# Gates of two branches computed beside their branch jobs, in one staging slot, with the head flips behind the last gate

## The chip, the cores and the metric

One core of a Trainium2 chip runs the whole program. The metric is the device time of one execution in microseconds, here the median of three. An execution with the hardware profiler gives the trace from which all rows come.

## The reference

A trunk of two layers over 768 tokens (two sequences of 256 and 512) with 1024 channels, all in float32. Of each layer, this is the part that matters here:

```python
proj = rms_norm(x, norm1_g) @ w_in            # q/k/v of three mixers, and gate_pre
o_a = dilated window attention(proj)          # 384 wide
o_b = bidirectional mLSTM(proj)               # 512 wide
o_c = rms_norm(differential attention(proj))  # 512 wide, 4 heads of 128, in two sequences
gates = sigmoid(gate_pre).reshape(Bn, S, 3, 1024)
y_a, y_b, y_c = o_a @ w_branch[:384], o_b @ w_branch[384:896], o_c @ w_branch[896:]
mixed = gates[:, :, 0] * y_a + gates[:, :, 1] * y_b + gates[:, :, 2] * y_c
x = x + mixed @ w_out
x = x + (silu(hg) * hu) @ w_ffn_out           # hg, hu = split(rms_norm(x) @ w_ffn_in)
```

## The kernel before

Every float32 product is made of three matmuls on rounded parts: high by high, high by low, low by high. `wh` and `wl` hold the parts of weights, `xh`, `xl` and `oh`, `ol` those of activations (transposed: channels on partitions, tokens along the row). ScalarE makes the high part by a copy (L1080), VectorE the low one by a subtraction (L1357); weights come in sub-chunks of 512 KB through three raw buffers `wraw`, issued by SyncE.

The work of a layer is a list `STEPS`, made by `schedule()` before the program is built. Each engine goes through the same list and does its share of each step, so the list is the order on every engine. It mixes two kinds of steps.

*Dense steps* are the large products. Each takes one of three PSUM banks in turn (L1758 to L1760 for the matmuls). `piece` steps are the projections; `gate b d q` is the product for block d (128 channels) of branch b's gate, for half q (384 tokens), 24 matmuls, which ScalarE turns into a sigmoid by three activations (L1089 to L1091) in one of three slots of `stage`; `branch b d q` is the product of branch b's output with its rows of w_branch, 9 matmuls for b = 0, 12 for the others; `turn 1 t` transposes token tile t of the mLSTM output, loaded by `turn_load` into a half of `wide`; `wout t h` is the last product.

*Side steps* are the small ones of the mixers, on the other five banks. `schedule()` puts one in when enough dense cost has gone by since the last (the `GAP` numbers). For the differential attention a unit is one tile of 128 queries of one head: `c_score` (L1975), a maximum on VectorE (L1651), two exponentials on ScalarE (L1264), `c_mix` (L1659 to L1662), `c_turn` (L1985), `c_out` (L1997). A head is opened by `c_fold` (L1961, transposes of q and k) and closed by `c_norm` (L1672 to L1680). `c_flip` (L2006) transposes the normed head into the operand of branch 2, in `xh[:, 4:8]`, whose rest VectorE makes (L1687). It overwrites the normalized input of the layer, so no flip may come before the last gate.

All 48 gate jobs stand ahead of the branch jobs, the last 32 of them beside mLSTM and differential units. Each gate is stored to `gate_t` in HBM by GpSimd's queue (L821). Of the branch jobs, those of branches 0 and 1 do this: GpSimd loads the gate back (`load_gate`, L840), VectorE multiplies the bank by it in place (L1423), GpSimd stores the product to `mix_t` (L870), for branch 1 as an accumulating store. Five slots serve for it (`gated`). In branch 2 the product is summed with the part loaded from `mix_t` (`load_part`, L851, three slots; L1430), and ScalarE and VectorE split the sum for w_out (L1147, L1410). `x` itself is loaded back from `x_save` (L880) for the last eight jobs of branch 2. GpSimd's queue is in order, so a load behind a wait holds all that follow:

```python
elif i >= GSLOTS:
    wait_mix_stored(i - GSLOTS)
```

In `mix(step)` of job i, `load_gate(i + 4)` is called first, so it waits for the store of job i - 1 to have landed.

## Time and profile before

| | us |
|---|---|
| median of three executions (3585.18 to 3595.86) | 3586.19 |
| the profiled execution | 3596.83 |
| its span, first to last instruction | 3595.2 |
| TensorE busy in the span | 3224.1 |
| VectorE, ScalarE, GpSimd busy | 1572.4, 1170.7, 508.5 |
| mean granted share of TensorE's clock | 0.96 |

Busy time is the time in which an engine carries out instructions. A wait is written down for the instruction that stood behind it, with the instruction or transfer that ended it. The layer loop runs twice, so most things stand in the trace twice.

### The profile page before, as it was taken

How to read it: one execution, taken by the hardware profiler on the slowest of the kernel's cores; microseconds unless marked ns; L12 is line 12 of the kernel's file. 1: busy time of each engine (PE TensorE's matmuls, PEld its weight loads, DVE VectorE, ACT ScalarE, POOL GpSimd, SP SyncE). 2: the span in 40 equal slices, each digit the busy share in tenths (PEclk: the TensorE clock that was granted, in tenths of full speed). 3: DMA queues.
4: the chain of work that ended last, by engine and by line, in shares of the span. 5: the costliest groups of instructions: out<-in, count | busy, mean ns of one | idle time of the engine just before them, and what ended most of it. 6: DMA issues, size and time to landing. Idle time of an engine off the chain costs nothing. (4 is left out here: it accounts for less than half of the span.)

```text
span 3595.2 us, 45725 instructions
## 1 busy us (share of the span) xinstructions
PE 3224.1 (90%) x17652; PEld 2940.5 (82%) x17652; DVE 1572.4 (44%) x3225; ACT 1170.7 (33%) x2480; POOL 508.5 (14%) x872
## 2 busy tenths in 40 slices
PE   6799998999866999999978899989998669999998
PEld 6788888787765899999877898877877658999997
DVE  5345245644433334434464442466444243344434
ACT  4334334455511221111143334344555112111111
POOL 0111312221223000000001113222112230000000
PEclk9999999999988999999989999999999889999999
DMA  3434443442256122112033344434323561122111
GB/s 126 136 100 131 126 141 111 126 120 88 88 144 168 47 71 71 55 50 70 30 122 107 107 135 123 139 114 121 115 93 102 133 176 36 59 70 70 58 47 65
DMA packets 273368, 358.63 MB, mean 100 GB/s; under 512 B 27440, under 2 KB 209904, under 8 KB 273176
## 3 DMA queue, kind: packets, MB, share of 16 engines
q1 hardware_dynamic: 214520, 182.59, 17.2%
q0 software_dynamic: 58656, 173.50, 15.7%
q8 instruction: 118, 1.93, 0.2%
q14 instruction: 74, 0.61, 0.1%
HBM read 264.42 MB, written 91.59 MB: 99 GB/s over the span
## 5 line engine op out<-in xcount | busy, mean ns | idle before, releaser
L1758 PE MATMUL ps<-wh,xh 128*128 128x384 f32 (+1 forms) x1440 | 543.8, 378 | 11.2 <-DVE wl L1357 6.6
L1759 PE MATMUL ps<-wl,xh 128*128 128x384 f32 (+1 forms) x1440 | 524.2, 364 | 0.0
L1760 PE MATMUL ps<-wh,xl 128*128 128x384 f32 (+1 forms) x1440 | 524.1, 364 | 0.0
L1758 PE MATMUL ps<-xh,wh 128*128 128x384 f32 (+1 forms) x1184 | 424.1, 358 | 111.3 <-DVE stage L1430 49.6
L1760 PE MATMUL ps<-xh,wl 128*128 128x384 f32 (+1 forms) x1184 | 408.6, 345 | 0.0
L1759 PE MATMUL ps<-xl,wh 128*128 128x384 f32 (+1 forms) x1184 | 408.5, 345 | 0.0
L1357 DVE TENSOR_TENSOR wl<-wraw,wh 128x1024 fp32r<-128x1024 f32 (+2 forms) x210 | 232.5, 1112 | 401.1 <-ACT wh L1080 400.6
L1832 PE MATMUL ps<-xh,wh 128*128 128x384 f32 x1408 | 361.4, 337 | 20.1 <-DVE arena L1745 15.4
L1832 PE MATMUL ps<-xl,wh 128*128 128x384 f32 x1408 | 359.0, 336 | 0.0
L1832 PE MATMUL ps<-xh,wl 128*128 128x384 f32 x1408 | 358.7, 335 | 0.0
L1758 PEld LDWEIGHTS ps<-xh,wh 128*128 128x128 f32 (+1 forms) x1184 | 229.1, 194 | 132.7 <-DVE stage L1423 55.0
L1758 PEld LDWEIGHTS ps<-wh,xh 128*128 128x128 f32 x1440 | 279.9, 194 | 41.5 <-DVE wl L1357 6.7
L1718 DVE SCALAR_TENSOR_TENSOR arena<-arena,ps 128x768 f32<-128x768 f32 x44 | 42.0, 955 | 601.5 <-ACT arena L1319 601.5
L1759 PEld LDWEIGHTS ps<-wl,xh 128*128 128x128 f32 x1440 | 279.1, 194 | 23.7 <-issue 1.4
L1760 PEld LDWEIGHTS ps<-wh,xl 128*128 128x128 f32 x1440 | 277.5, 193 | 25.1
L1832 PEld LDWEIGHTS ps<-xh,wh 128*128 128x128 f32 x1408 | 254.6, 189 | 28.4 <-issue 20.5
L1832 PEld LDWEIGHTS ps<-xl,wh 128*128 128x128 f32 x1408 | 255.8, 189 | 0.0
L1832 PEld LDWEIGHTS ps<-xh,wl 128*128 128x128 f32 x1408 | 255.7, 189 | 0.0
L1760 PE MATMUL ps<-wh,ol 128*128 128x512 f32 x624 | 243.2, 390 | 0.0
L1759 PE MATMUL ps<-wl,oh 128*128 128x512 f32 x624 | 243.1, 390 | 0.0
L1758 PE MATMUL ps<-wh,oh 128*128 128x512 f32 x624 | 242.7, 389 | 0.0
L1319 ACT ACTIVATE arena<-ps 128x768 f32<-128x768 f32 x44 | 35.8, 815 | 615.3 <-PE ps L1832 615.3
(223 smaller groups left out, 5020.5 us busy)
## 6 DMA issues: line engine op xcount, KB each, us to landing
wraw<-in_w_in SPq DMA_DIRECT2D x96, 512.0 KB, 3.8
wraw<-in_w_ffn_in SPq DMA_DIRECT2D x88, 512.0 KB, 4.0
wraw<-in_w_in SPq DMA_DIRECT2D x72, 384.0 KB, 3.6
wraw<-in_w_ffn_out SPq DMA_DIRECT2D x44, 512.0 KB, 3.3
qkv_a<-stage POOLq DMA_DIRECT2D x108, 192.0 KB, 2.2
gate_t<-stage POOLq DMA_DIRECT2D x96, 192.0 KB, 2.2
stage<-gate_t POOLq DMA_DIRECT2D x78, 192.0 KB, 2.7
mix_t<-stage POOLq DMA_DIRECT2D x52, 192.0 KB, 3.6
```

The lines of the kernel that those rows point to most:

```text
L1319: act.activation(f_e[:, ft, :].rearrange("p (h n) -> p h n", h=2), ps[:, 4 * ft:4 * ft + 2, 0:HALF_TOK], ACT.Tanh, scale=0.5).then_inc(f_e ...
L1357: dve.tensor_tensor(wl[:, half, j, 0:w], wraw[:, n % RAW, 0:w], wh[:, half, j, 0:w].bitcast(F32), ALU.subtract).then_inc(w_lo, 1)
L1718: fch.link(dve.scalar_tensor_tensor(e2, e2, 1.0, ps[:, 4 * ft:4 * ft + 2, 0:HALF_TOK], ALU.add, ALU.mult))
L1758: pe.matmul(out, ah, bh, start=first, stop=False)
L1759: pe.matmul(out, ah, bl, start=False, stop=False)
L1760: return pe.matmul(out, al, bh, start=False, stop=last)
L1832: mm = pe.matmul(pair[0:cols, q, 0:HALF_TOK], w[:, half, j, sl_], v[:, k, q * HALF_TOK:(q + 1) * HALF_TOK], start=(k == 0 and w is wh and ...
```

## The change

It orders and places work anew; all products, sigmoids and sums are the same.

1. The gates of branch 2 are computed first, where those of branch 0 were, and stored to `gate_t`, which keeps one branch instead of three. The gates of branches 0 and 1 are not stored: job i's gate is computed, two gates later comes its branch job, and VectorE multiplies the bank by the gate in the staging slot itself. The product is stored to `mix_t` from there, and the slot's next gate waits for this store. Weights come in `mix` chunks of two gate sub-chunks and one of the branch.
2. The turns of branch 1 go to `oh`, `ol` in place of branch 0's operand, behind its last job, since `xh`, `xl` are needed by the gates; they stand in two groups of three.
3. All eight flips follow the last gate, in groups of three, three and two, in four side banks; the heads' outputs get places of their own in the arena. The square of `c_norm` goes to PSUM (`AT_OUT`), so the next head's first `c_out` waits for the reduction of it.
4. Branch 2 has five slots for parts. The first five gates are loaded behind the last `c_norm`, the first five parts during branch 1; `x` is loaded back in its first six jobs, in two groups of three tiles.
5. `GAP_C` is 3.7 instead of 4, and w_out is taken second half first.

```diff
-    gates = [("gate", [("in", 0, 8, COL_GATE + (4 * i + j) * P, P) for j in range(4)]) for i in range(6)]
-    chunks += gates[0:2]
+    gate = lambda b, d: ("in", 0, 8, COL_GATE + (KD * b + d) * P, P)
+    for i in range(2):
+        chunks.append(("gate", [gate(2, 4 * i + j) for j in range(4)]))
     for i in range(3):
         chunks.append(("c", [("in", 2 * j, 2, COL_C + i * C_W, C_W) for j in range(4)]))
-    chunks += gates[2:6]
-    for b, parts in ((0, ((0, 1), (2, 3))), (1, (range(4),)), (2, (range(4),))):
-        for part in parts:
-            chunks.append(("branch", [("branch", *MIX_ROWS[b], 2 * j * P, 2 * P) for j in part]))
-    for h in range(2):
+    for b in range(2):
+        for i in range(4):
+            chunks.append(("mix", [gate(b, 2 * i), gate(b, 2 * i + 1), ("branch", *MIX_ROWS[b], 2 * i * P, 2 * P)]))
+    chunks.append(("branch", [("branch", *MIX_ROWS[2], 2 * j * P, 2 * P) for j in range(4)]))
+    for h in (1, 0):
         chunks.append(("out", [("wout", 2 * j, 2, h * 512, 512) for j in range(4)]))
     return chunks
...
-    if kind == "gate":
-        return C_GATE[(8 * s[1] + s[2]) // 4], s[2] % 4
-    if kind == "branch":
-        b, j = s[1], s[2] // 2
-        return (C_BRANCH + j // 2, j % 2) if b == 0 else (C_BRANCH + 1 + b, j)
+    if kind in ("gate", "branch"):
+        b, d = s[1:3]
+        if b < 2:
+            return C_MIX + 4 * b + d // 2, d % 2 if kind == "gate" else 2
+        return (C_GATE + d // 4, d % 4) if kind == "gate" else (C_BRANCH, d // 2)
     if kind == "wout":
-        return C_OUT + s[2], None
+        return C_OUT + 1 - s[2], None
...
-GAP_A, GAP_B, GAP_C, ROUND = (1, 2, 4, 2.5), (4, 4, 6), 4, 0.45
+GAP_A, GAP_B, GAP_C, ROUND = (1, 2, 4, 2.5), (4, 4, 6), 3.7, 0.45
...
-    dense += [("gate", 0, d, q) for d in range(KD) for q in range(2)]
+    dense += [("gate", 2, d, q) for d in range(KD) for q in range(2)]
     dense += [("piece", c, t) for c in range(C_C, C_C + 3) for t in range(NT)]
-    dense += [("gate", b, d, q) for b in (1, 2) for d in range(KD) for q in range(2)]
-    for d in range(KD):
-        dense += [("branch", 0, d, q) for q in range(2)]
-        if d < NT:
-            dense.append(("turn", 1, d))
-        if d + 2 < NT:
-            dense.append(("turn_load", 1, d + 2))
-    dense += [("branch", 1, d, q) for d in range(KD) for q in range(2)]
+    jobs = [(d, q) for d in range(KD) for q in range(2)]
+    for b in range(2):
+        for i in range(len(jobs) + 2):
+            if i < len(jobs):
+                dense.append(("gate", b, *jobs[i]))
+                if b == 1 and i < 2:
+                    for t in range(3 * i, 3 * i + 3):
+                        dense.append(("turn", 1, t))
+                        if t + 2 < NT:
+                            dense.append(("turn_load", 1, t + 2))
+            if i >= 2:
+                dense.append(("branch", b, *jobs[i - 2]))
     dense += [("branch", 2, d, q) for q in (1, 0) for d in range(KD)]
...
-        if flips and flips[0] in normed and ("gate", 2, KD - 1, 1) in gone and (
+        if flips and flips[0] in normed and ("gate", 1, KD - 1, 1) in gone and ("c_norm", 7) in gone and (
                 len(dense_of(steps)) > max(normed[flips[0]], flipped) or not dense or not side and dense[0] == ("branch", 2, 0, 0)):
             steps.append(("c_flip", flips.pop(0)))
             gone.add(steps[-1])
-            flipped = len(dense_of(steps))
+            if flips and flips[0] % 3 == 0:
+                flipped = len(dense_of(steps))
             continue
...
+                        if step[0] == "gate" and step[1] < 2:
+                            return
...
-                        if m == len(STAGED) - 1:
-                            wait_stage(m)
-                            for i in range(GSLOTS - 1):
-                                load_gate(i)
-
-                    def wait_mix_stored(i):
-
-                        pool.wait_ge(mix_stored[i % GSLOTS], 16 * (i // GSLOTS + 1))
-
-                    def load_gate(i):
-
-                        _, b, d, q = MIX_LIST[i]
-                        if i - GSLOTS >= MIX_LAST:
-                            pool.wait_ge(r_lo, i - GSLOTS - MIX_LAST + 1)
-                        elif i >= GSLOTS:
-                            wait_mix_stored(i - GSLOTS)
-                        elif i == GSLOTS - 1:
-                            pool.wait_ge(b_dec, len(B_UNITS))
-                        pool.dma_start(gated[i % GSLOTS], gate_t[b, d * P:(d + 1) * P, HALVES[q]]
-                                       ).then_inc(gate_in[i % GSLOTS], 16)
+
+                    def load_gate(j):
+
+                        _, b, d, q = MIX_LIST[MIX_LAST + j]
+                        if j >= GSLOTS:
+                            pool.wait_ge(r_lo, j - GSLOTS + 1)
+                        pool.dma_start(gated[j % GSLOTS], gate_t[d * P:(d + 1) * P, HALVES[q]]).then_inc(gate_in[j % GSLOTS], 16)
...
+
+                    def first_gates():
+
+                        stage_stored(STAGE["gate", 2, KD - 1, 1])
+                        pool.wait_ge(c_tr, len(C_FOLDS))
+                        pool.wait_ge(c_ptr, len(C_UNITS))
+                        pool.wait_ge(c_pv, len(C_UNITS))
+                        for j in range(GSLOTS):
+                            load_gate(j)
+
+                    parts = []
+
+                    def first_parts(ready):
+
+                        while len(parts) < PSLOTS and 2 * len(parts) + 1 <= ready:
+                            load_part(len(parts))
+                            parts.append(ready)
 
...
+                        pool.wait_ge(mixed, i + 1)
                         if b < 2:
-                            pool.wait_ge(mixed, i + 1)
+                            m = STAGE["gate", b, d, q]
                             if b:
-                                wait_mix_stored(MIXES["branch", 0, d, q])
+                                stage_stored(STAGE["gate", 0, d, q])
                             add = {"accum_op": ALU.add} if b else {}
-                            pool.dma_start(mix_t[d * P:(d + 1) * P, HALVES[q]], gated[i % GSLOTS], **add
-                                           ).then_inc(mix_stored[i % GSLOTS], 16)
+                            pool.dma_start(mix_t[d * P:(d + 1) * P, HALVES[q]], stage[:, m % SLOTS, 0:HALF_TOK], **add
+                                           ).then_inc(stored[m % SLOTS], 16)
+                            if b and STEPS.index(("c_norm", 7)) < STEPS.index(step):
+                                first_parts(i - 2 * KD - 2)
                             return
                         j = i - MIX_LAST
-                        if j + PSLOTS - 1 < 2 * KD:
-                            load_part(j + PSLOTS - 1)
-                        if KD <= j < KD + NT:
-                            t = FFN_TILES[j - KD]
-                            if j == KD:
-                                pool.wait_ge(c_flo, len(C_HEADS))
-                            pool.dma_start(x[:, t, :], x_save[t * P:(t + 1) * P, :]).then_inc(x_back, 16)
+                        if j == 0:
+                            first_parts(2 * KD)
+                            pool.wait_ge(c_flo, len(C_HEADS))
+                        if j + PSLOTS < 2 * KD:
+                            load_part(j + PSLOTS)
+                        if 1 <= j and j - 1 + GSLOTS < 2 * KD:
+                            load_gate(j - 1 + GSLOTS)
+                        if j < NT:
+                            t = FFN_TILES[j]
+                            pool.dma_start(x[:, t, :], x_save[t * P:(t + 1) * P, :]).then_inc(x_back[j // 3], 16)
...
+                        elif kind == "c_norm" and step[1] + 1 == len(C_HEADS):
+                            first_gates()
                         elif kind == "turn_load":
                             load_turn(*step[1:])
+                        elif kind == "turn" and step[1:] == (1, NT - 1):
+                            pool.wait_ge(d_done, INDEX["turn", 1, NT - 1] + 1)
+                            pool.dma_start(wide[:, :], io["norm2_g"][layer].partition_broadcast(P)
+                                           ).then_inc(gain2_in, 16)
...
                         elif kind == "branch":
                             i = MIXES[step]
-                            e = gated[i % GSLOTS]
-                            dve.wait_ge(gate_in[i % GSLOTS], 16 * (i // GSLOTS + 1))
+                            j = i - MIX_LAST
+                            if j < 0:
+                                g = ("gate", *step[1:])
+                                e = stage[:, STAGE[g] % SLOTS, 0:HALF_TOK]
+                                dve.wait_ge(act_staged, PLAIN[g] + 1)
+                            else:
+                                e = gated[j % GSLOTS]
+                                dve.wait_ge(gate_in[j % GSLOTS], 16 * (j // GSLOTS + 1))
                             dve.wait_ge(d_done, n + 1)
                             ins = dve.tensor_tensor(e, ps_bank(n)[:, 0:HALF_TOK], e, ALU.mult)
-                            if i < MIX_LAST:
+                            if j < 0:
                                 ins.then_inc(mixed, 1)
                             else:
-                                j = i - MIX_LAST
                                 chain.link(ins)
                                 dve.wait_ge(part_in[j % PSLOTS], 16 * (j // PSLOTS + 1))
                                 dve.tensor_tensor(e, e, part_mix[j % PSLOTS], ALU.add).then_inc(mixed, 1)
...
                             dve.wait_ge(c_pv, C_LAST[H] + 1)
-                            if H >= 4:
-                                dve.wait_ge(c_fl, H - 3)
                             chain.link(dve.reciprocal(unit_s[:, 44:44 + n], c_z[:, H % 3, 0:n]))
                             dve.tensor_tensor(o, side[:, AT_OUT:AT_OUT + n * P].rearrange("p (t e) -> p t e", t=n),
                                               spread(unit_s[:, 44:44 + n]), ALU.mult).then_inc(c_ov, 1)
                             dve.wait_ge(co_sq, H + 1)
-                            dve.tensor_reduce(unit_s[:, 48:48 + n], c_tmp[:, 0:n * P].rearrange("p (h e) -> p h e", e=P), AX_X,
+                            dve.tensor_reduce(unit_s[:, 48:48 + n], side[:, AT_OUT:AT_OUT + n * P].rearrange("p (h e) -> p h e", e=P), AX_X,
                                               ALU.add).then_inc(co_ss, 1)
                             dve.wait_ge(co_rs, H + 1)
...
                             if H and t == 0:
-                                pe.wait_ge(c_ov, H)
+                                pe.wait_ge(co_ss, H)
...
                             pe.wait_ge(co_n, H + 1)
-                            flip_bank_free(pe, step)
+                            if H == 0:
+                                pe.wait_ge(c_ex, 2 * len(C_UNITS))
+                                pe.wait_ge(c_pt, len(C_UNITS))
+                                pe.wait_ge(co_ss, len(C_HEADS))
+                            if H >= 4:
+                                pe.wait_ge(c_flo, H - 3)
                             for t in range(n):
-                                mm = pe.transpose(side[:, AT_FOLD + t * P:AT_FOLD + (t + 1) * P], c_o[:, H % 4, t, :],
-                                                  ident[:, :])
+                                mm = pe.transpose(flip_bank(H)[:, t * P:(t + 1) * P], c_o[H][:, t, :], ident[:, :])
                             mm.then_inc(c_fl, 1)
```

Two places in the orders of the engines. First GpSimd's queue at the end of branch 1 and the start of branch 2, before; `stage` and `arena` hold the gates there, L840 are their loads, L870 the stores of products, L851 the parts.

```order
L840 DMA arena<-gate_t 128x384
L870 DMA mix_t<-stage 128x384
L840 DMA stage<-gate_t 128x384
L870 DMA mix_t<-stage 128x384
L851 DMA arena<-mix_t 128x384 x2
L861 ISA
L861 DMA wide<-in_norm_g 128x1024
L840 DMA stage<-gate_t 128x384
L851 DMA arena<-mix_t 128x384
```

In the changed program the same place reads as follows; L873 are the stores of products, L836 the loads of branch 2's gates, L844 the parts, L888 the tiles of x.

```order
L873 DMA mix_t<-stage 128x384 x2
L836 DMA arena<-gate_t 128x384 x5
L873 DMA mix_t<-stage 128x384
L844 DMA arena<-mix_t 128x384 x3
L873 DMA mix_t<-stage 128x384 x2
L844 DMA arena<-mix_t 128x384
L873 DMA mix_t<-stage 128x384 x2
L844 DMA arena<-mix_t 128x384
L873 DMA mix_t<-stage 128x384 x4
L844 DMA arena<-mix_t 128x384
L888 DMA arena<-x_save 128x1024
L844 DMA arena<-mix_t 128x384
L836 DMA arena<-gate_t 128x384
```

The gate loads ahead of each store are gone; the loads of gates and parts for branch 2 stand between the stores of branch 1, and x follows the first job of branch 2 instead of the ninth.

Second, TensorE's order at the turns, whose operand is `wide`. Before, the first turn, between branch jobs of branch 0, flips and a unit:

```order
L2006 MATMUL ps<-ident,arena 128x128 x4
L1814 MATMUL ps<-ident,wide 128x128 x4
L2006 MATMUL ps<-ident,arena 128x128 x4
L1975 MATMUL ps<-arena 128x256 x2
L1985 MATMUL ps<-ident,arena 128x128 x2
L1997 MATMUL ps<-arena 128x128 x2
```

In the changed program the first group stands between two units of the differential attention (L1993 the scores, L2003 and L2015 its turn and output, L1979 a fold):

```order
L1993 MATMUL ps<-arena 128x512 x2
L2003 MATMUL ps<-ident,arena 128x128 x4
L2015 MATMUL ps<-arena 128x128 x4
L1979 MATMUL ps<-ident,arena 128x128 x4
L1830 MATMUL ps<-ident,wide 128x128 x12
L1993 MATMUL ps<-arena 128x512 x2
L2003 MATMUL ps<-ident,arena 128x128 x4
```

Three turns of four transposes have become one run of twelve. The second and third load of `wide` follow the first and second turn in GpSimd's queue.

## Rows read from the trace of the kernel before

**Rows 1.** The page, busy time and share of the span.

```profile
PE 3224.1 (90%) x17652; PEld 2940.5 (82%) x17652; DVE 1572.4 (44%) x3225; ACT 1170.7 (33%) x2480; POOL 508.5 (14%) x872
```

**Rows 2.** TensorE, waits of the whole run: who for whom; us, times, longest.

```profile
PE ps L1758 <- DVE stage L1430: 51.1, 11, 19.8
...
PE ps L1758 <- DVE stage L1423: 46.4, 22, 4.4
...
PE ps L1975 <- ACT arena L1264: 20.3, 22, 2.0
...
PE ps L1758 <- DVE arena L1423: 12.6, 8, 3.9
...
PE ps L2006 <- DVE arena L1680: 11.0, 4, 3.5
...
PE ps L1961 <- DMA arena<-qkv_c: 9.7, 2, 4.8
PE ps L2006 <- DVE xl L1687: 8.1, 6, 2.5
...
PE ps L1961 <- DVE xl L1687: 5.2, 2, 2.6
...
PE ps L1758 <- DVE arena L1430: 2.6, 2, 1.5
```

**Rows 3.** Stretches: length, PE, PEld, DVE, ACT, POOL busy, PEclk, DMA share, GB/s.

```profile
808.00:967.00 159.00, 146.25 (x870) 125.99 (x869) 71.18 (x125) 87.81 (x207) 26.50 (x42) 0.99 0.26 81
967.00:1040.00 73.00, 57.10 (x303) 52.32 (x302) 35.91 (x72) 24.17 (x53) 22.26 (x41) 0.88 0.54 164
1040.00:1121.00 81.00, 37.51 (x156) 33.05 (x156) 11.20 (x17) 0.00 (x0) 25.13 (x36) 0.77 0.54 103
1121.00:1160.00 39.00, 31.70 (x155) 29.82 (x156) 24.03 (x43) 10.64 (x17) 16.57 (x32) 0.91 0.71 231
2521.00:2945.00 424.00, 341.19 (x1875) 302.88 (x1874) 176.71 (x331) 166.17 (x368) 105.99 (x174) 0.93 0.43 120
```

**Rows 4.** Timeline of TensorE in branch 2 (start, length).

```profile
1121.65 0.69 PE L1758 MATMUL ps<-xh,wh 128*128 128x384 f32 x1 [19.83 <-DVE stage L1430]
...
1130.86 0.44 PE L1758 MATMUL ps<-xh,wh 128*128 128x384 f32 x1 [0.95 <-DVE stage L1430]
...
1134.97 0.34 PE L1760 MATMUL ps<-xh,wl 128*128 128x384 f32 x1
```

**Rows 5.** Timeline of GpSimd in branch 1.

```profile
1096.18 0.56 POOL L840 DMA_DIRECT2D stage<-gate_t  x1 [3.67 <-DMA mix_t<-stage]
1096.72 0.89 POOL L870 DMA_DIRECT2D mix_t<-stage  x1
1101.10 0.57 POOL L840 DMA_DIRECT2D stage<-gate_t  x1 [3.49 <-DMA mix_t<-stage]
```

**Rows 6.** Timeline of VectorE, the product of a branch-2 job.

```profile
1124.27 0.55 DVE L1423 TENSOR_TENSOR stage<-ps,stage 128x384 f32<-128x384 f32 x1
```

**Rows 7.** DMA issues of the branch stretches, median us to landing.

```profile
mix_t<-stage POOLq DMA_DIRECT2D x26, 192.0 KB, 3.6
...
wide<-o_tok POOLq DMA_DIRECT2D x4, 256.0 KB, 3.6
```

**Rows 8.** Timeline of GpSimd at the first fold.

```profile
791.29 0.56 POOL L821 DMA_DIRECT2D gate_t<-stage  x1 [6.71 <-ACT stage L1091]
```

**Rows 9.** Timeline beside one unit of the differential attention.

```profile
870.33 0.69 ACT L1264 ACTIVATE arena<-ps,c_s 128x512 f32<-128x512 f32 x1 [2.25 <-DVE c_s L1651]
...
872.15 0.50 ACT L1089 ACTIVATE stage<-ps 128x384 f32<-128x384 f32 x1
...
873.67 1.04 ACT L1080 ACTIVATE wh<-wraw 128x1024 fp32r<-128x1024 f32 x1
...
874.74 1.23 DVE L1357 TENSOR_TENSOR wl<-wraw,wh 128x1024 fp32r<-128x1024 f32 x1 [4.44 <-ACT wh L1080]
...
877.00 1.22 DVE L1651 TENSOR_REDUCE c_s<-ps 128x2 f32<-128x1024 f32 x1
...
878.25 0.69 ACT L1264 ACTIVATE arena<-ps,c_s 128x512 f32<-128x512 f32 x1 [3.54 <-DVE c_s L1651]
```

**Rows 10.** Stretch with loads of x in flight.

```profile
1150.00:1155.00 5.00, 2.26 (x14) 1.94 (x13) 1.26 (x3) 0.53 (x1) 1.17 (x3) 1.00 1.01 374
```

More of the change, by code:

```diff
@@ L60 @@
 GSLOTS = 5
-PSLOTS = 3
+PSLOTS = 5
 SUB = 1024
@@ L297, in side_needs @@
         return ("piece", C_C + 2, NT - 1)
-    if kind == "c_norm" and s[1] >= 4:
-        return ("c_flip", s[1] - 4)
     return None
@@ L363, in schedule @@
             steps.append(("ffn_split",))
-        if done < NT and i >= WOUT.index((FFN_TILES[done], 1)):
+        if done < NT and i >= WOUT_END[FFN_TILES[done]]:
             steps.append(("rms", NT + done))
@@ L382 @@
 STAGE = {s: m for m, s in enumerate(STAGED)}
-FLIP_BANK = [s for s in STEPS if s[0] in ("c_fold", "c_flip")]
 MIXES = {s: i for i, s in enumerate([s for s in DENSE if s[0] == "branch"])}
@@ L519, in build @@
         b_og = area("b", 4 * P).rearrange("p (t e) -> p t e", t=4)
+        b_o = area("b", 4 * P).rearrange("p (t e) -> p t e", t=4)
+        early = used["bg"] = used["b"]
+        b_w = area("b", 2 * B_W).rearrange("p (i h e) -> p i h e", i=2, h=B_H)
+        b_u = area("b", 4 * P)
+        b_q = area("b", 4 * P)
+        b_k = area("b", 4 * P)
+        b_c = area("b", 4 * P + 2)
         b_d = area("b", 2 * 10 * P).rearrange("p (d n) -> p d n", d=2)
-        b_o = area("b", 4 * P).rearrange("p (t e) -> p t e", t=4)
         b_nb = area("b", 2 * 2 * 4 * P).rearrange("p (r d n) -> p r d n", r=2, d=2)
@@ L559, in build @@
         stored = [sem(f"stored{i}") for i in range(SLOTS)]
-        mix_stored = [sem(f"mix_stored{i}") for i in range(GSLOTS)]
         gate_in = [sem(f"gate_in{i}") for i in range(GSLOTS)]
@@ L564, in build @@
         n_rstd, n_xn, n_tr, n_hi, n_lo = (sem(x) for x in ("n_rstd", "n_xn", "n_tr", "n_hi", "n_lo"))
-        x_saved, x_back = sem("x_saved"), sem("x_back")
+        x_saved, x_back = sem("x_saved"), [sem(f"x_back{i}") for i in range(2)]
         t_in = [sem(f"t_in{i}") for i in range(2)]
@@ L655, in build, with flip_bank @@
         AT_TURN, AT_OUT, AT_FOLD = 1024, 1536, 2048
-        def flip_bank_free(eng, step):
-            before = [s[0] for s in FLIP_BANK[:FLIP_BANK.index(step)]]
-            if "c_fold" in before:
-                eng.wait_ge(c_qkt, before.count("c_fold"))
-            if "c_flip" in before:
-                eng.wait_ge(c_flo, before.count("c_flip"))
+        def flip_bank(H):
+            return side[:, 512 * (H % 4):512 * (H % 4 + 1)]
         def mix_rows(hi, d):
@@ L856, in mix @@
                         i = MIXES[step]
-                        if b == 2 and i == MIX_LAST:
-                            for r in range(PSLOTS - 1):
-                                load_part(r)
-                            pool.wait_ge(d_done, INDEX["turn", 1, NT - 1] + 1)
-                            pool.dma_start(wide[:, :], io["norm2_g"][layer].partition_broadcast(P)
-                                           ).then_inc(gain2_in, 16)
-                        if i + GSLOTS - 1 < len(MIXES):
-                            load_gate(i + GSLOTS - 1)
+                        pool.wait_ge(mixed, i + 1)
@@ L1956, in side_step @@
                             pe.wait_ge(c_lin, 32 * (H + 1))
-                            flip_bank_free(pe, step)
+                            i = C_FOLDS.index(step)
+                            if i:
+                                pe.wait_ge(c_qkt, i)
                             at = AT_FOLD
```

82 lines of the change are left out of this document (39 added, 43 removed).

## Prediction

> **What bounds the kernel now.** I read the page's busy shares first: TensorE 3224 of 3595 us, no other engine over half [rows 1]. So the time is TensorE's work plus the 371 us in which it does nothing, and the question is which of these idle stretches the change reaches. The wait table of TensorE for the whole run lists them by what ended them [rows 2]. Two lines belong to the branch jobs: the wait for L1423 (product of a bank and a gate; 46.4 + 12.6 us) and for L1430 (sum with the part loaded back; 51.1 + 2.6 us). That is 113 us. Then 19.1 us before head flips (L2006), 5.2 us of a fold (L1961) behind a flip's rest in the same bank, 9.7 us of a fold behind a load of qkv_c, 20.3 us of score jobs behind the exponentials of the unit before.
>
> Next I cut one layer into stretches [rows 3]. Idle time is length minus PE busy: 12.8 us in the gates beside differential units, then 15.9, 43.5 and 7.3 us in the three stretches of branch jobs, 79 us; with half of the 9.7 us above it is 84 for the stretch that the change reorders. Layer 2 in one row: 424.0 - 341.2 = 83. The granted clock falls as well: 0.88, 0.77 and 0.91 in the branch stretches against 0.99 ahead of them. The wait of 1121.65 us (19.8 us long) and the rows behind it show what TensorE does at full speed: 24 matmuls from 1130.86 to 1134.97, a step of 0.179 us, so 12 matmuls (a branch job of 4 row blocks) are 2.15 us, 9 are 1.6 and a gate's 24 are 4.3 [rows 4].
>
> Why the branch jobs wait is in GpSimd's queue [rows 5]. Ahead of each product it issues the load of a gate into a slot whose mix store must have landed (3.5 us of idle time before each load), then the next store. One job passes every 4.9 us (1096.18 to 1101.10) where TensorE needs 2.15.
>
> **What is removed.** Branches 0 and 1 get their gate from a staging slot that ScalarE filled one or two jobs earlier; the 32 gate stores, the 32 gate loads and the load-behind-store loop are gone in each layer. The jobs of the loop now have a gate job of 4.3 us between them, so a pair takes 6.4 us of TensorE against a chain of product 0.55, issue 0.6 to 0.9 and landing 3.6 [rows 5 to 7]. I remove the 113 us of L1423 and L1430. The 19.8 us wait goes with them: it was the last accumulating stores, read back by the first parts. Parts 0 to 4 are now requested between branch-1 jobs.
>
> Flips: eight in four banks behind the last gate. Their heads are normed long before, and no fold shares their bank. Of 19.1 + 5.2 us I take away 22; the fifth flip still waits for the first one's rest.
>
> Fold behind its load: in the program's order GpSimd asks for qkv_c right behind a gate store, and this store, of 791.29, waited 6.7 us for the sigmoid [rows 8]. That store no longer exists, and the product that stands in its place comes earlier. 9.7 us go.
>
> Slow clock: the three branch stretches hold 57.1 + 37.5 + 31.7 = 126.3 us of busy time [rows 3]. Their 48 branch jobs have 528 matmuls, 94.5 us at 0.179, and the turns, flips and last unit pieces some 9 (an estimate from their counts at the 0.1 to 0.3 us that such pieces take): 23 us a layer are slow clock and restarts. With gates between the jobs I let 8 remain: -15 a layer, -30.
>
> **What is added.** (a) Turns of branch 1: they stood one between two pairs of branch jobs each; now they stand in two groups of three, and `wide` has two halves. The third of a group waits for a load that GpSimd issues only when the first is done. Issue to landing is 3.6 us for such a load [rows 7], less the 0.5 us of the turn between and plus a semaphore: 3.3 us, four times: +13. The Trainium skill ("DMA: Bandwidth & Descriptors", section on the anatomy of one DMA) gives about 2.0 us plus bytes over 436 GB/s, for 256 KB an estimate of 2.6 us; by it this term would be +9. The row is used.
>
> (b) Units of the differential attention beside shorter jobs. The loop that can hold them is in [rows 9]: exponentials at 870.33, sigmoid 872.15, weight split on ScalarE 873.67 and VectorE 874.74, maximum 877.00, next exponentials 878.25: 7.9 us. The score jobs that waited did so 20.3 / 22 = 0.9 us [rows 2], so TensorE's own work in such a period is 7.0: a gate of 4.3 and a unit of 2.7. In the branch-0 part a unit now has a gate and a branch job beside it (8.6 us), which covers the loop. In the branch-1 part units stand alternately beside a gate and beside a branch job of 2.15 us. Only 3 sub-chunks are split for 8 jobs there; about five splits fall beside gates (0.9 each) and one beside a branch job, where the loop without a sigmoid but with a product is some 7.0 against 4.9 (2.1). That is 7 us a layer against today's 10; I add 8 a layer for the ends of heads, where the next head's first output product now waits for a reduction too, for the turns' evacuations and for slots: 5 a layer net, +10. Bounds: 0, and all 16 units of a layer at 7.9 instead of 4.3 / 2 + 2.15 / 2 + 2.7 = 5.9 us, +64.
>
> (c) Branch 2: gates, parts (five slots now) and the six x tiles (512 KB each) are all asked for in its first jobs. About 11 gates, 11 parts and 6 tiles are 7.4 MB, with 2 MB of w_out in the 34 us of its 16 jobs: 280 GB/s. The trace moves 374 GB/s with x tiles in the queue and 231 over the stretch [rows 3, 10]. By job 10 it must have some 5.7 MB + 1 MB in 21 us, 320 GB/s. I take +4 a layer, +8 (bounds 0 and, at 231 GB/s, 8 us a layer). The staging slots cost nothing on TensorE: the gate that reuses a slot ends 4.3 us after the branch job, the store lands 0.55 + 0.2 + 3.6 us after it, so ScalarE waits some tenths, and TensorE wants the gate's bank 6.4 us later.
>
> Edits at nothing: gate 2 in gate 0's early place, the halves of w_out exchanged, other arena places (same bytes); the square in PSUM (0.6 us before, hidden like now).
>
> **The sum.** -113 - 22 - 10 - 30 + 13 + 10 + 8 = -144; I give back 6 for new small starts between 64 alternating jobs: -138. The profiled execution took 3596.8 us (span 3595.2), 10.6 over the median of 3586.2; so 3459 profiled and 3448 as median.
>
> **Rivals.** *The unit loop binds* (7%): short jobs leave every unit of the branch-1 part to the chain of [rows 9], slot waits of ScalarE lengthen it. Speaks for it that maximum and exponentials stand in one order with split and sigmoid; against, that only three splits fall to eight jobs. +60: 3508.
>
> *The clock stays low* (8%). TensorE's granted clock was 0.99 in the stretch of gates and units with 11 short waits of score jobs (22 in both layers [rows 2]) and 0.77 where it waited 3.5 us at every job [rows 3, 5]. If many short waits were enough, the 30 us would not come back and the gates would lose as much again: +50, 3498. The Trainium skill has such a rule ("TensorE: Matmul & The Clock Gate", on the second failure mode): frequent short idling between groups of matmuls makes the clock swing. The row of 0.99 with 12.8 us of short waits does not bear it out here.
>
> *Everything overlaps* (8%): turns' loads and x tiles are hidden, the clock returns whole: 3448 - 35 = 3413.
>
> *Slower: three slots are too few* (2%). A slot now holds a gate through sigmoid, waiting, product and store. If the landing came so late that ScalarE passed 4 us of wait on to TensorE's bank, every gate of branches 0 and 1 would be held; with 64 gates it decides from 138 / 64 = 2.2 us each, a landing of about 10 us. The rows have 3.6. At 3 us each: 3448 + 192 = 3640.
>
> *It moves nothing* (2%): the idle time turns up again in front of branch 2; 3586.
>
> **The numbers.** The forecast has 73%, its own range 3425 to 3475 from the bounds of (a), (b), (c) and the clock. The range for 8 in 10 takes in the clock rival: 3418 to 3498. A measurement of this kernel tells some 0.3% (11 us) from no change. Faster 0.96, same 0.02, slower 0.02.
>
> **What would show it.** Right: the L1423 wait under 10 us, L1430 under 15, granted clock above 0.95 from the first gate of branch 0 to w_out, waits of the turns on `wide` of 3 us, four of them. Wrong: score jobs waiting for exponentials over 60 us in total (unit loop), a clock under 0.9 without long waits, sigmoids waiting for slots with TensorE's gates behind them.

## The result, and the profile after

The changed kernel takes 3504.16 us (median of four runs, 3503.35 to 3505.1), the kernel before 3585.68 beside it: a ratio of 0.9767, 95% interval 0.9749 to 0.9785. The prediction was 3448 us with a range of 3418 to 3498. The sign and the terms removed were right, the gain was 82 us and not 138, and the time lies 6 us outside the range. The profiled execution took 3503.35 us, the one of before 3596.8: 93.5 us by the two traces.

The page of the changed kernel, the row of busy times:

```profile
PE 3213.1 (92%) x17652; PEld 2936.1 (84%) x17652; DVE 1568.7 (45%) x3225; ACT 1168.7 (33%) x2480; POOL 438.1 (13%) x744
```

The span is 3501.7 us. Beside [rows 1] TensorE is idle for 288.6 us instead of 371.1 (-82.5) and busy for 11 us less. The prediction had 108 us less idle time (all its terms but the clock) and 30 us less busy time. TensorE's waits in the whole run of the changed kernel (who for whom; us, times, longest):

```profile
PE ps L1993 <- ACT arena L1278: 39.7, 16, 4.6
PE ps L1965 <- DVE arena L1615: 29.5, 10, 4.6
...
PE ps L1830 <- DMA wide<-o_tok: 13.0, 4, 3.6
...
PE ps L1950 <- ACT arena L1226: 7.1, 3, 3.3
PE ps L1774 <- ACT stage L1105: 6.8, 4, 2.7
...
PE ps L2029 <- DVE xl L1703: 5.6, 3, 2.8
...
PE ps L1774 <- DVE arena L1449: 3.6, 4, 1.5
PE ps L1774 <- DVE stage L1443: 3.4, 5, 1.3
```

Against [rows 2] (its L1423 and L1430 are now L1443 and L1449): the 113 us of branch jobs are 7.0 (the last two rows), the head flips' 19.1 us are 5.6, the fold behind its load is gone, the turns wait 13.0 us as computed. New or longer are the score jobs (L1993, 39.7 instead of 20.3), the mLSTM's output and score jobs (L1965 29.5, L1950 7.1) and jobs that wait for a gate's last activation (L1105, 6.8). All of these wait for ScalarE or VectorE, so I asked what ScalarE waits for. Its waits in the changed kernel:

```profile
ACT stage L1103 <- DMA mix_t<-stage: 135.1, 26, 9.8
ACT arena L1278 <- DVE c_s L1669: 120.5, 40, 5.3
```

A sigmoid (L1103 is its first activation) waits 26 times, 5.2 us on average, until the mix store of its staging slot has landed. The prediction gave this "some tenths". Such a wait begins when ScalarE runs idle, which can be before the gate's bank is ready; counted from when the bank was ready and ScalarE free, the 26 sigmoids are 105 us late, 4.0 on average. The exponentials wait 120.5 us for the maximum. In the kernel before, the same view has no first row, and of the second

```profile
ACT arena L1264 <- DVE c_s L1651: 89.0, 36, 3.5
```

One of the waits for a landing can be followed through four queues. The timeline of the changed kernel (start, length, in brackets the idle time before and who ended it), rows of TensorE's dense jobs left out:

```profile
820.14 0.55 DVE L1443 TENSOR_TENSOR stage<-ps,stage 128x384 f32<-128x384 f32 x1
820.51 0.76 POOL L1045 DMA_DIRECT2D o_tok<-arena  x1 [9.22 <-DVE arena L1648]
822.24 0.56 DVE L1443 TENSOR_TENSOR stage<-ps,stage 128x384 f32<-128x384 f32 x1 [0.42 <-PE ps L1776]
...
823.55 1.09 POOL L998 DMA_DIRECT2D wide<-o_tok  x2 [2.28 <-DMA o_tok<-arena]
...
824.64 1.08 POOL L873 DMA_DIRECT2D mix_t<-stage  x2
...
827.78 0.49 ACT L1103 ACTIVATE stage<-ps 128x384 f32<-128x384 f32 x1 [9.74 <-DMA mix_t<-stage]
...
829.29 0.67 ACT L1278 ACTIVATE arena<-ps,c_s 128x512 f32<-128x512 f32 x1
...
830.86 2.08 PE L1993 MATMUL ps<-arena 64*128 64x512 f32 x4 [4.57 <-ACT arena L1278]
...
832.60 1.04 ACT L1094 ACTIVATE wh<-wraw 128x1024 fp32r<-128x1024 f32 x1
...
833.67 1.23 DVE L1371 TENSOR_TENSOR wl<-wraw,wh 128x1024 fp32r<-128x1024 f32 x1 [10.88 <-ACT wh L1094]
...
835.93 1.22 DVE L1669 TENSOR_REDUCE c_s<-ps 128x2 f32<-128x1024 f32 x1
837.07 0.55 DVE L1443 TENSOR_TENSOR stage<-ps,stage 128x384 f32<-128x384 f32 x1
837.18 0.69 ACT L1278 ACTIVATE arena<-ps,c_s 128x512 f32<-128x512 f32 x1 [3.54 <-DVE c_s L1669]
```

The slot that the sigmoid at 827.78 needs is that of the product at 820.14, whose branch job had ended at 814.76: VectorE had the steps of the mLSTM's output ahead of it. The stores of both products then stand in GpSimd's queue behind the store of that output (820.51) and the loads of two turns, and these loads wait for the output to land. So the mix stores go from 824.64 on, the sigmoid starts at 827.78, the exponentials queued behind it at 829.29, and TensorE's score job has waited 4.57 us. It goes on from there: ScalarE's half of a weight split (L1094) stands behind the sigmoids, VectorE's rest of it (L1371) has waited 10.88 us for that half, and behind the rest stand the maximum of the next unit and the next product. The product's store is what a later sigmoid waits for. By this order it can go in a circle: landing, sigmoid, split, rest, product, store, landing; and the maximum with the exponentials hangs on the same two queues. How much each part costs is for the experiments.

The clock: stretches of the changed kernel (length, PE busy, further engines, PEclk, DMA share, GB/s).

```profile
900.00:1000.00 100.00, 86.81 (x472) 72.95 (x470) 47.47 (x90) 48.06 (x122) 15.51 (x21) 0.86 0.26 64
...
1077.00:1111.00 34.00, 32.24 (x184) 31.43 (x183) 25.79 (x46) 11.14 (x18) 14.98 (x28) 1.00 0.85 285
```

In the stretch 900:1000, turns and units with branch-1 gates, TensorE waits 12.7 us (four score jobs up to 3.2 us, one turn 3.6 us) and is granted 0.86. Inside it:

```profile
905.00:910.00 5.00, 5.00 (x31) 4.43 (x29) 2.23 (x4) 2.88 (x7) 1.43 (x2) 1.00 0.18 52
910.00:917.40 7.40, 3.83 (x28) 2.90 (x24) 4.58 (x7) 4.99 (x13) 1.29 (x2) 0.84 0.23 71
917.40:921.80 4.40, 4.40 (x16) 2.84 (x16) 3.65 (x7) 1.23 (x3) 0.55 (x1) 0.50 0.36 117
```

Busy without a gap TensorE has 1.00; it waits 3.57 us for a turn's load (until 916.44), the clock of 910:917.4 is 0.84, and at 917.4:921.8 it is at 0.50, the level of 1.2 GHz. Over the whole of the reordered part, 731:1111, it is 0.93, where the prediction's sign of being right was above 0.95. Branch 2 (1077:1111) is at 1.00 with 285 GB/s.

### The profile page after: what moved, and what is told of

The parts are those of the page before. It is cut to its first block and busy times, and to the rows that moved or that the text cites. A ratio compares the mean times of both kernels' runs of the same rounds, so it can differ in the third digit from the quotient of the medians.

```text
span 3501.7 us, 45591 instructions
## 1 busy us (share of the span) xinstructions
PE 3213.1 (92%) x17652; PEld 2936.1 (84%) x17652; DVE 1568.7 (45%) x3225; ACT 1168.7 (33%) x2480; POOL 438.1 (13%) x744
## 5 line engine op out<-in xcount | busy, mean ns | idle before, releaser
L1371 DVE TENSOR_TENSOR wl<-wraw,wh 128x1024 fp32r<-128x1024 f32 (+2 forms) x210 | 232.5, 1112 | 484.1 <-ACT wh L1094 483.5
L1774 PE MATMUL ps<-xh,wh 128*128 128x384 f32 (+1 forms) x1056 | 363.2, 344 | 7.0 <-DVE arena L1449 3.6
L1775 PE MATMUL ps<-xl,wh 128*128 128x384 f32 (+1 forms) x1056 | 356.4, 337 | 0.0
L1776 PE MATMUL ps<-xh,wl 128*128 128x384 f32 (+1 forms) x1056 | 356.3, 337 | 0.0
L1776 PEld LDWEIGHTS ps<-wh,xl 128*128 128x128 f32 x1440 | 277.3, 193 | 24.6
L1094 ACT ACTIVATE wh<-wraw 128x1024 fp32r<-128x1024 f32 (+2 forms) x210 | 199.7, 958 | 39.1 <-DMA wraw<-in_w_in 28.2
```

Source lines behind the costliest of these rows:

```text
L1094: act.activation(wh[:, half, j, 0:w], wraw[:, n % RAW, 0:w], ACT.Copy).then_inc(w_hi, 1)
L1371: dve.tensor_tensor(wl[:, half, j, 0:w], wraw[:, n % RAW, 0:w], wh[:, half, j, 0:w].bitcast(F32), ALU.subtract).then_inc(w_lo, 1)
L1774: pe.matmul(out, ah, bh, start=first, stop=False)
L1775: pe.matmul(out, ah, bl, start=False, stop=False)
L1776: return pe.matmul(out, al, bh, start=False, stop=last)
```

## The experiments

All times are medians of four runs; the ratio is to runs of the kernel before on the same chip, which took 3586 to 3599 us, so kernels are compared by ratio. "Landing" is ScalarE's wait L1103 for mix stores, "maximum" its wait for c_s, "score" TensorE's wait for exponentials, "busy" TensorE's (us, whole run, line numbers shift with the edit). No interval that is not shown is wider than 0.004.

| kernel | us | ratio | landing | maximum | score | busy |
|---|---|---|---|---|---|---|
| before | 3586 | 1 | - | 89.0 | 20.3 | 3224.1 |
| changed | 3504.2 | 0.9767 | 135.1 | 120.5 | 39.7 | 3213.1 |
| e1 four slots | 3455.7 | 0.9623 | 9.7 | 124.4 | 35.3 | 3187.0 |
| e2 turns in pairs | 3486.3 | 0.9706 | 133.6 | 128.1 | 31.5 | 3197.4 |
| e3 gap 4 | 3479.1 | 0.9689 | 154.4 | 97.7 | 25.8 | 3193.4 |
| e4 = e1 + e2 | 3450.3 | 0.9605 | 8.1 | 132.2 | 24.6 | 3187.1 |
| e5 rests later | 3440.2 | 0.957 | 103.3 | 86.7 | 20.0 | 3190.4 |
| e6 = e1 + pairs ahead | 3431.5 | 0.9543 | 8.0 | 123.7 | 30.3 | 3183.0 |
| e7 = e1 + e3 | 3438.3 | 0.9567 | 9.5 | 104.0 | 9.6 | 3182.6 |
| e10 = e1 + e5 | 3410.4 | 0.9478 | 7.8 | 87.3 | 10.7 | 3182.9 |
| e8 = e6 + e5 | 3393.8 | 0.9438 | 8.0 | 88.3 | 11.3 | 3169.8 |
| e11 = e6 + all rests | 3406.7 | 0.9465 | 8.0 | 87.1 | 11.5 | 3180.7 |
| e12 = e10 + e3 | 3419.8 | 0.9511 | 9.6 | 43.6 | 3.5 | 3182.0 |
| e9 before + rests later | 3576.0 | 0.9926 | - | 38.7 | none | 3225.9 |

**e1, four slots.** The gates of branches 0 and 1 take four places of 384 numbers in the memory of the three places of 512.

`M0` is the number of the first gate of branch 0, `MSLOTS` is 4. The edit, cut (`...`):

```
+        def slot_of(m):
+
+            if m < M0:
+                return stage[:, m % SLOTS, :]
+            return stage_rows[:, (m - M0) % MSLOTS * HALF_TOK:((m - M0) % MSLOTS + 1) * HALF_TOK]
...
-                        if m >= SLOTS:
-                            act.wait_ge(stored[m % SLOTS], 16 * (m // SLOTS))
-                        return stage[:, m % SLOTS, :]
+                        wait_free(act, m)
+                        return slot_of(m)
```

> The gates of branches 0 and 1 get four staging places of 384 numbers instead of three of 512 (same memory). In the changed kernel ScalarE waits 135 us (26 times) in front of a sigmoid for the landing of a mix store, and TensorE waits 39.7 us for exponentials queued behind. Theory 'slots': the landing waits fall under 40 us, the score jobs' wait falls from 39.7 to about 20 as before the change, the 6.8 us of jobs waiting for a gate's last activation go, and some 10 us of slow clock come back: about 3470 us. Rival 'unit loop': the loop of exponentials, maximum and weight split beside short jobs sets the score waits, so they stay at 35 to 40 us although the landing waits go: 3495 to 3505 us.

The ratio is 0.9623 (0.9598 to 0.9648), 1.5% below the changed kernel and more than expected. But the score jobs' wait hardly fell. TensorE's waits for exponentials and for turns in this kernel:

```profile
PE ps L2020 <- ACT arena L1305: 35.3, 18, 3.5
...
PE ps L1857 <- DMA wide<-o_tok: 12.9, 4, 3.6
```

Of some 51 us by the two traces, 25 are idle time (the waits of the jobs for a last activation, of the mLSTM's scores and of flips, 6.8 + 6.5 + 5.6, and 4.4 of the score jobs) and 26 are busy time with the same matmuls, while the mean granted clock rose from 0.964 to 0.971. So the slots cost, but the rival is right on the score jobs: something else holds them.

**e2 and e4, turns in pairs** behind the first three gates, with three slots and with four.

```
-                if b == 1 and i < 2:
-                    for t in range(3 * i, 3 * i + 3):
+                if b == 1 and i < 3:
+                    for t in range(2 * i, 2 * i + 2):
```

> The six turns of branch 1 stand in three pairs behind the first three gates instead of two groups of three, so no turn needs a load that is issued only just before it. Theory 'turns': the 13.0 us of waits on wide go, and with them the slow clock behind two of them (about 3 us a layer): 3504 - 13 - 6 = 3485 us. Rival: the wait hides others (the score jobs behind the turns stand in the unit loop anyway), so their waits grow by as much and the time stays within 4 us of 3504.

> Four staging places and the turns in pairs together. If both theories ('slots' and 'turns') hold and their stretches don't overlap, the gains add up: 3504 - 34 - 19 = 3451 us, with the granted clock of the stretch of branch-1 gates at 0.95 or more where it was 0.86. If the unit loop binds instead, 3485 to 3504 us with that clock under 0.9.

The waits on `wide` went, as worked out, and another came that I had not foreseen. TensorE in e4, then ScalarE and VectorE ahead of it:

```profile
907.99 1.04 PE L1857 MATMUL ps<-ident,wide 128*128 128x128 f32 x8
918.27 0.66 PE L1801 MATMUL ps<-oh,wh 128*128 128x384 f32 x1 [9.24 <-issue]
...
915.42 1.06 ACT L1194 ACTIVATE oh<-ps 128x512 fp32r<-128x512 f32 x2
...
916.89 1.28 DVE L1485 TENSOR_TENSOR ol<-ps,oh 128x512 fp32r<-128x512 f32 x2
```

The first branch job stood right behind the last pair and waited 9.2 us a layer for its copies into `oh` and `ol`, which stood behind a head's norm on both engines. e2 gained 0.6% net; e4 over e1 has 0.2%, which the intervals don't tell from nothing. Both came within 1.5 us of their theories (3485 and 3451), but by luck. In e2 13.0 us of waits on `wide` went and 18.5 us came; what made the gain is 15.7 us less busy time and 8.2 us less wait of score jobs. In e4 the slots gave more than the 34 us put down for them and the turns less than 19, and the clock at 900:1000 is 0.91, not 0.95.

**e3, the gap between units back to 4.0** (`GAP_C`, one number).

> Only the gap between units of the differential attention goes back from 3.7 to 4.0, so each unit of the branch-1 part has a gate and a branch job beside it (8.6 us with its own 2.2 to 2.7) and the last units end seven jobs later, just ahead of branch 2. Theory 'short jobs' (units beside a branch job of 2.15 us alone are what makes score jobs wait): score waits fall from 39.7 to under 25 us, against it the last flips stand close to the first jobs of branch 2 and cost up to 8 us: about 3495 us. Theory 'slots': slots are held as long as before, score waits stay over 32 us, the late flips cost: 3505 to 3515 us.

Neither was right: score waits fell to 25.8, just short of the first theory's mark, while the landing waits rose to 154.4 us in 40 waits, and flips waited 8.2 us (5.6 in the changed kernel). The time was 16 us below what the better theory gave; busy time fell by 20 us.

**e5, rests later.** Three slots. On VectorE alone, the rest of a weight split that stood behind a gate of branch 0 or 1 goes behind the next job:

```
+REST_AT = {}
+for s_, list_ in SPLITS.items():
+    mixed_job = s_[0] in ("gate", "branch") and s_[1] < 2 and DENSE[INDEX[s_] + 1][0] in ("branch", "gate")
+    REST_AT.setdefault(DENSE[INDEX[s_] + 1] if mixed_job and s_[0] == "gate" and s_ in STAGE and s_[1] < 2 else s_, []).extend(list_)
...
-                            for c, n in SPLITS.get(step, []):
+                            for c, n in REST_AT.get(step, []):
```

> Three places as in the changed kernel; only on VectorE the rest of a weight split that stood right behind a gate of branch 0 or 1 now stands behind the next job, so the product of a branch job no longer queues behind a rest that waits for ScalarE's half of the split. Theory 'circle' (the sigmoid waits for a landing, ScalarE's split waits behind the sigmoid, VectorE's rest waits for that split, and the next product with its store waits behind the rest): the landing waits of ScalarE fall from 135 us to under 60 and the time to 3465 to 3480 us with three places. Rival 'places only' (with three places the landing is late whatever VectorE's order is): the landing waits stay over 110 us, the time within 8 us of 3504.

This small edit gave more than the slots: 0.957 (0.9548 to 0.9593). Landing waits fell only to 103.3, between the two theories. But counted as above, from when bank and ScalarE were ready, the sigmoids are 55 us late instead of 105, and a branch job's product starts 1.4 us behind its job instead of 3.1 (means of 64). So the circle was there, and the edit opened it. Of the 55 us, 34 are two waits a layer of 8 to 9 us, those behind the mLSTM's output, which are as long in the changed kernel and have no rest in them. What fell as well is the wait for the maximum. A unit beside a weight split in e5, VectorE and ScalarE:

```profile
865.79 1.23 DVE L1674 TENSOR_REDUCE c_s<-ps 128x2 f32<-128x1024 f32 x1 [3.49 <-PE ps L1998]
869.37 0.56 DVE L1448 TENSOR_TENSOR stage<-ps,stage 128x384 f32<-128x384 f32 x1 [2.35 <-PE ps L1781]
869.84 1.22 DVE L1376 TENSOR_TENSOR wl<-wraw,wh 128x1024 fp32r<-128x1024 f32 x1
...
864.78 0.49 ACT L1108 ACTIVATE stage<-ps 128x384 f32<-128x384 f32 x1 [4.04 <-PE ps L1781]
...
866.29 1.04 ACT L1099 ACTIVATE wh<-wraw 128x1024 fp32r<-128x1024 f32 x1
867.24 0.67 ACT L1283 ACTIVATE arena<-ps,c_s 128x512 f32<-128x512 f32 x1
```

The maximum now waits for TensorE alone and runs beside sigmoid and split; the exponentials follow the split with no gap, where the changed kernel had 3.54 us (837.18). The rest comes last and waits for nobody.

**e10, both.**

> Four places and later rests without a change of the turns: the fourth corner beside 3504 (neither), 3456 (places), 3440 (rests). If the two act on one loop (sigmoid waits for a landing, split behind it, rest behind the split, product and maximum behind the rest), the gains of 49 and 64 us overlap: 3415 to 3425 us, as the kernel with pairs ahead too took 3394. If they were independent it would be 3504 - 49 - 64 = 3391 us.

0.9478 (0.946 to 0.9497). From 0.9767 the slots took 0.0144, the rests 0.0197, both 0.0289: 0.005 (18 us) of the two is shared, less than I thought, and with four intervals in this sum it is uncertain by 0.004. Mostly each has its own share. With four slots the rests still take the maximum waits from 124.4 to 87.3 and the score waits from 35.3 to 10.7, while the landing waits, 9.7 already, hardly change.

**e6 and e8, pairs of turns ahead of the gates**, with four slots, and with later rests too. A gate and a unit now stand between the last pair and the first branch job.

```
+            if b == 1 and i < 3:
+                for t in range(2 * i, 2 * i + 2):
+                    dense.append(("turn", 1, t))
+                    if t + 2 < NT:
+                        dense.append(("turn_load", 1, t + 2))
             if i < len(jobs):
                 dense.append(("gate", b, *jobs[i]))
-                if b == 1 and i < 2:
-                    for t in range(3 * i, 3 * i + 3):
-                        dense.append(("turn", 1, t))
-                        if t + 2 < NT:
-                            dense.append(("turn_load", 1, t + 2))
```

> Four places, and the turns of branch 1 in three pairs, each AHEAD of one of the first three gates, so that a gate and a unit lie between the last pair and the first branch job (behind the gates, the first branch job waited 9.2 us in each layer for the last pair's copies, which stood behind a head's norm on ScalarE and VectorE). Theory: the 12.9 us of waits on wide go and no 9.2 us wait comes: 3456 - 13 - 5 = 3438 us. Rival 'unit loop': the score jobs behind the turns wait instead, 3446 to 3456 us.

> Four places, pairs of turns ahead of the gates, and the rests of the weight splits one job later on VectorE. If VectorE's order still delays maxima and with them exponentials once the places are enough, some 5 to 10 us more come off: about 3430 us. If the circle is all that the order did, it closes no more with four places and the time is that of the kernel with four places and pairs ahead, within 4 us.

e6 is at 0.9543, 0.8% below e1, as the theory of the turns gave it: by the two traces 13 us of waits on `wide`, 5 of score jobs, 4 of busy time, less some small waits. e8 is at 0.9438 (0.9422 to 0.9454), 3393.8 us: 3.4% below the changed kernel, the fastest of all. The rests took 38 us here, more than the 5 to 10 expected. The changed kernel and e8 from the first gate of branch 0 on:

```profile
731.00:1090.00 359.00, 319.71 (x1769) 284.94 (x1768) 160.84 (x304) 159.97 (x358) 63.27 (x96) 0.93 0.34 93
...
731.00:1090.00 359.00, 350.83 (x2042) 315.54 (x2041) 192.63 (x352) 177.06 (x387) 71.25 (x110) 1.00 0.43 120
```

**e7 and e12, gap 4.0 with four slots, and with later rests.**

> Four places and the gap between units of 4.0. If the 35 us of score waits that are left with four places come from units beside a branch job of 2.15 us alone, they fall to about 20 and the time to about 3440 us; the late flips (8 us of waits with three places) take some of it back: 3440 to 3448. If the gap only helped because longer periods covered the landing waits, which four places remove, the time stays at 3452 to 3460 us.

> Four places, later rests, and the gap between units of 4.0 (turns in two groups of three as in the changed kernel). With three places, and with four, the gap took 0.6 to 0.8% off. Theory 'the short jobs cost only through the loop': with the rests out of it 10.7 us of score waits are left and the gap can give back at most half of them, less what the late flips cost (6 to 8 us): ratio to the kernel before within 0.002 of 0.948 (four places and later rests alone). Rival 'a unit beside a short job costs by itself': it again takes 0.5% or more off, a ratio of 0.943 or less.

With four slots (e7) the longer gap took score waits down to 9.6 us, further than the 20 that I had put down. The longer gap took 0.8% off the changed kernel, 0.6% off four slots, and nothing once the rests were later: 0.9511 (0.9479 to 0.9542) beside 0.9478, a difference that the intervals don't tell apart. Its score waits are down to 3.5 us, but flips wait 6.2 us and branch jobs 6.7 (none and 3.3 in e10), which more than takes those 7 us back. So a cost of units beside short jobs that is not the rest's is at most these few us.

**e11, every rest later.**

> Four places, pairs ahead, and every rest of the layer ahead of w_out one job later on VectorE, those behind pieces and branch jobs too (the kernel with 3394 us moves only those behind gates of branches 0 and 1). The theory that the rest must stand out of the way of what TensorE waits for gives some of the 25.6 us of output jobs of the mLSTM, 27.7 us of the dilated turns and 11.3 us of score jobs: 3375 to 3390 us. Rival: those waits have their own causes, and weights arrive later for the next chunk: 3394 us or more.

0.9465 against 0.9438, so no gain, more likely a loss: the mLSTM's output jobs waited 17.5 us instead of 25.6, but jobs waited 23.7 us for `wl` (6.5 in e8). Which rest is moved matters.

**e9, the same edit in the kernel before**, there behind the gates of all three branches.

> The control in the kernel BEFORE the change: on VectorE the rest of a weight split behind a gate goes one job later there too, nothing else. Theory 'the change made VectorE's order costly' (shorter jobs beside the units, sigmoids that wait for a landing): before the change the score jobs waited only 20.3 us, so at most these and some clock come back: 3570 to 3586 us. Rival 'the order costs the same everywhere': the kernel before gains as much as the changed one did (64 us): about 3525 us.

0.9926 (0.9898 to 0.9954). All 20.3 us of score waits went, and idle time as a whole fell by as much (350.9 us instead of 371.1). Busy time did not fall (3225.9 beside 3224.1). So the order of VectorE's queue cost 0.7% before and 2.0% after the change: the change made it dear.

## Why the prediction was off, step by step

**Where the miss lies.** By the two traces the gain is 93.5 us and not 138: idle time fell by 82.5 instead of 108, busy time by 11 instead of 30. Some 11 us more of the median's miss come from the last line of the sum, which took off the 10.6 us by which the profiled execution of before stood above its median; that of the changed kernel stands 0.8 below its own.

**Right.** The branch jobs with branch 2 (c): -113 + 8 = -105 forecast, -105.7 by the rows, of whose 7.0 us left 3.6 wait for the sum with a part (L1449) and 3.4 for a product (L1443). 1077:1111, in branch 2, is 32.24 us busy of 34. Flips and the fold behind them: -22 forecast, -18.7 measured. Fold behind its load: -10, measured -9.7. The turns (a): +13 forecast, 13.0 measured in four waits up to 3.6 us, and e6 took them away. The estimate of 2.6 us per load from the Trainium skill ("DMA: Bandwidth & Descriptors", anatomy of one DMA) would have given +9; the rows of the trace were the better price.

**The step that failed** is in (c): "The staging slots cost nothing on TensorE", since the store would have landed 4.35 us behind the branch job. I added product, issue and landing as if each began when the one before ended. Measured from the job's last matmul, the stores of the changed kernel landed 7.3 us later (median of 64). VectorE started the product 3.1 us behind that matmul on average, with rests that wait for ScalarE, maxima or the mLSTM's output ahead of it; in 6 jobs of 64 the store waited over 1 us more behind GpSimd's other transfers. The slots put at nothing cost 51 us by the traces of e1.

**The second step that failed** is (b) at +10: score jobs, mLSTM jobs and last activations wait 37 us more than before (19.4 + 4.8 + 6.2 + 6.8). Only about half of that follows from the slots: e1 took 17.7 us of it away and left the score jobs at 35.3 us. These hang on the place of the rest: with it one job later (e5) they wait 20.0, as before the change. The loop of [rows 9] was the right one to look at, but I took over its order, with the rest ahead of the maximum, and let every sigmoid in it start on time.

**The clock: -30 forecast, -11 measured**, the largest miss beside (b). With e10's edits busy time is 41 us below before, with e8's 54. So the size of the term was in reach, and I think that the waits of 3 to 5 us that the loop left behind kept it away. That the changed kernel's variants with fewer waits have less busy time is measured; how the 26 us of e1 divide over single waits is not.

**The rivals.** "The unit loop binds" gave 3508 us, close to the 3504 measured, and named the slot waits of ScalarE as a part; it had 7% and deserved more, though the nearness of the time is partly luck. Its mark, score waits over 60 us, did not come (39.7), and its place was wrong: of the 60.6 us of landing waits in layer 1, 24.0 fall beside the mLSTM's last units (731:820), 11.8 in the rest of branch 0, 0.9 in 900:1000 and 23.9 behind it, where nearly no unit is left. "The clock stays low" was partly true: I held a row of 0.99 with 12.8 us of short idle time against it, but those waits were 2.0 us (one of 2.6) at most. With waits of 3.2 and 3.6 us the stretch of 900:1000, idle for as long, has 0.86. By the rule of the Trainium skill ("TensorE: Matmul & The Clock Gate", second failure mode) short idling between groups of matmuls makes the clock swing; the changed kernel agrees with it at 900:1000 (0.86), the kernel before at 808:967 does not (0.99).

**Left open.** GpSimd's order (the turns' loads ahead of two stores at 823.55) was not tried by itself, nor the mLSTM's output ahead of a product on VectorE; the four waits behind them are 34 of the 105 us by which sigmoids are late, and four slots hide them. Nor was the clock separated from the waits.

## What to carry to other kernels

When a change reuses a buffer sooner, don't add the durations of its chain: walk it through each engine's queue and ask at every link what stands ahead and what that waits for. An instruction that waits for another engine (here the rest of a weight split) belongs behind everything in its queue that TensorE will want first; here moving it one job back was worth 2.0% for no memory and no work. Look in the other engines' wait tables too: TensorE's showed 39.7 us, ScalarE's 135 and 120. But such a wait is idle time and not lateness: for 30 of the 135 us the sigmoid's own bank was not ready either.

## What was unexpected in the hardware

Matmuls at 905:910 had 1.00; with a single wait of 3.57 us, which ended at 916.44, the clock fell, and it was at 0.50 until 921.8. Over a whole run, four slots took 25 us of idle time away and 26 us of busy time, with the same 17652 matmuls. But the two don't go together at a fixed rate: later rests took 40 and 23 us off the changed kernel, pairs of turns (e2) 2 and 16, and later rests in the kernel before, where the score waits were 2.0 us at most, 20 us of idle time and no busy time.

A store of 192 KB to `mix_t` landed 2.1 to 4.0 us after its issue in branch 0 and 3.3 to 5.5 us in branch 1, where it is an accumulating store. The prediction had one number, 3.6, for both.
